# Fewer stages around the latent heads, a norm inside the projections, and a state space whose spans run two chunks ahead

## What is computed

```
# block one, state space mixer, 8 chunks of 128 tokens, 8 heads of 64
Lmat = exp(segsum(A))                                   # "spans"
y_diag = einsum(Cc, Bc, Lmat, X); y_off = einsum(Cc, prev, exp(a_cum))
y = (y_diag + y_off + d_skip * xs) * silu(z)
y = y * rsqrt(mean(y^2) + eps) * norm_w
# block two, run twice (2 layers)
xn = rms_norm(h, attn_norm); proj = xn @ w_in           # 1024 x 2208
q = (rms_norm(c_q, q_norm) @ w_uq)                      # latent attention, 6 heads of 64 + 32
kv = (rms_norm(c_kv, kv_norm) @ w_ukv)
q_pe = apply_rope(q[..., 64:]); o_b = softmax(q k^T * scale) v
h = h + concat(rms_norm(o_a), rms_norm(o_b), rms_norm(o_c)) * gn @ w_out
h = h + expert_choice_ffn(rms_norm(h, ffn_norm), ...)
```

## Time and profile before

| | us |
|---|---|
| median of 3 runs | 4294.49 |
| range of the runs | 4283.99 to 4298.66 |
| the profiled execution, own time | 4293.83 |
| its span | 4292.1 |
| PE busy | 3480.9 (81%) |
| DVE busy | 2808.4 (65%) |
| ACT busy | 1915.9 (45%) |
| mean granted clock of PE | 0.898 of full |

### The profile page before, as it was taken

One profiled execution on the slowest core, in us unless ns is written; L12 is line 12 of the kernel. 1 busy time (PEld: TensorE's weight loads), 2 busy tenths in 40 slices (PEclk: granted clock), 3 DMA queues, 4 the chain that ended last, 5 costly groups with the idle time before them and its releaser, 6 DMA issues. The chain is left out here.

```text
span 4292.1 us, 54019 instructions
## 1 busy us (share of the span) xinstructions
PE 3480.9 (81%) x18170; PEld 2563.5 (60%) x18170; DVE 2808.4 (65%) x4432; ACT 1915.9 (45%) x3024; POOL 513.8 (12%) x353
## 2 busy tenths in 40 slices
PE   7991559858880999698939999959978985799995
PEld 3440336746660786366828888848654664688884
DVE  1798346469995318365389999822554655899995
ACT  0100235126653126344327777622453531677774
POOL 0001200015553100100001111100001000011110
PEclk9995669969995999899969999979988997899997
DMA  3000000346624210001249999821100023799996
GB/s 120 23 0 11 6 1 2 109 187 260 253 88 171 77 50 3 20 1 60 104 164 376 384 385 385 334 97 49 27 10 11 1 96 126 281 384 383 383 384 242
DMA packets 122011, 649.31 MB, mean 151 GB/s; under 512 B 14176, under 2 KB 22752, under 8 KB 69856
## 3 DMA queue, kind: packets, MB, share of 16 engines
q1 hardware_dynamic: 101376, 572.44, 34.4%
q0 software_dynamic: 15984, 58.20, 4.7%
q10 hardware_dynamic: 4464, 16.25, 0.9%
HBM read 584.46 MB, written 62.39 MB: 151 GB/s over the span
## 5 line engine op out<-in xcount | busy, mean ns | idle before, releaser
L2950 DVE TENSOR_TENSOR low_ring<-mix,high_ring 128x2048 fp32r<-128x2048 f32 x256 | 576.6, 2284 | 41.3 <-ACT high_ring L2899 41.3
L2899 ACT ACTIVATE high_ring<-mix 128x2048 fp32r<-128x2048 f32 x256 | 477.8, 1937 | 130.8 <-PEq L122 130.8
L2840 PE MATMUL ps<-high_ring,x_high 128*128 128x512 f32 x1024 | 410.1, 400 | 14.9 <-DVE low_ring L2950 7.6
L2841 PE MATMUL ps<-low_ring,x_high 128*128 128x512 f32 x1024 | 401.1, 392 | 0.0
L2842 PE MATMUL ps<-high_ring,x_low 128*128 128x512 f32 x1024 | 400.6, 391 | 0.0
L2950 DVE TENSOR_TENSOR low_ring<-more_raw,high_ring 128x2048 fp32r<-128x2048 f32 x128 | 290.1, 2286 | 27.9 <-ACT high_ring L2899 27.9
L2899 ACT ACTIVATE high_ring<-more_raw 128x2048 fp32r<-128x2048 f32 x128 | 246.5, 1926 | 0.0
L2840 PEld LDWEIGHTS ps<-high_ring,x_high 128*128 128x128 f32 x1024 | 193.1, 189 | 78.9 <-DVE low_ring L2950 20.5
L2842 PEld LDWEIGHTS ps<-high_ring,x_low 128*128 128x128 f32 x1024 | 193.1, 189 | 41.4
L2841 PEld LDWEIGHTS ps<-low_ring,x_high 128*128 128x128 f32 x1024 | 193.3, 189 | 37.7
L2840 PE MATMUL ps<-high_ring,h_high 128*128 128x512 f32 x512 | 205.2, 401 | 0.0
(11 more groups left out here) (451 smaller groups left out, 8141.3 us busy)
## 6 DMA issues: line engine op xcount, KB each, us to landing
mix<-in_expert_units SPq DMA_DIRECT2D x256, 1024.0 KB, 8.0
more_raw<-in_expert_units SPq DMA_DIRECT2D x128, 1024.0 KB, 8.5
raw_experts<-in_expert_units SPq DMA_DIRECT2D x16, 3072.0 KB, 10.6
expert_out<-out ACTq DMA_DIRECT2D x31, 512.0 KB, 2.6
w_mix<-in_w_out SPq DMA_DIRECT2D x12, 1024.0 KB, 6.2
mix<-in_w_turned SPq DMA_DIRECT2D x20, 512.0 KB, 3.8
mix<-residual SPq DMA_DIRECT2D x8, 1024.0 KB, 8.2
mix<-residual SPq DMA_DIRECT2D x16, 512.0 KB, 3.3
```

The lines of the kernel that those rows point to most:

```text
L2840: nc.tensor.matmul(ps[:, bank, :], left_high, high, start=first, stop=False)
L2841: nc.tensor.matmul(ps[:, bank, :], left_high, low, start=False, stop=False)
L2899: nc.scalar.activation(w_high[:, n % RING, :], raw[n % RAW_UNITS], ACT.Copy).then_inc(high_ready, 1)
L2950: nc.vector.tensor_tensor(w_low[:, n % RING, :], raw[n % RAW_UNITS], w_high[:, n % RING, :].bitcast(F32), ALU.subtract).then_inc(low_ready, 1)
```

## The change

One edit in each of these places:

- State space: PE makes the spans of chunk c + 2 at the end of chunk c, and the pairs' first part of chunk c + 1 at its start; DVE writes `a_upto` two chunks ahead and `pairs` (now two buffers) one chunk ahead; the state product comes ahead of the outer one. The gates' Silu moves to ACT's start in `convolve`, the gating product and the square into the chunk loop, and the separate last stage goes.
- `project_two` takes in the norm, the transposes and the split: rows come tile by tile into the place of `feats`, each tile is squared, rooted, scaled by root and a gain row, turned, and split. Groups of the first two units are interleaved so that the first two need only tiles 0 to 3.
- `latent_heads` replaces five stages: norm, transposes, products for q, k and v and the rotary turn of q, in two halves of 512 tokens, over six PSUM banks, with all its DMAs issued at its start.
- `mix_out_square`: the gain row and the first two weight units are loaded during `attend_latent`, into the upper part of the old `qk` tile (now split in `body` and `tail`); the first weight unit is split ahead of the second tile's norm. There and in `mix_out_norm` the first product group waits for the first weight unit at its start and for the second only halfway (`halfway`).

```diff
-def split_products(nc, out, pairs):
+def split_products(nc, out, pairs, halfway=None):
...
+        if halfway is not None and 2 * n == len(terms):
+            halfway()
...
-                pe.wait_ge(low_ready, 2 * h + 2)
+                pe.wait_ge(low_ready, 2 * h + 1)
```

On ACT in `convolve`; on PE and on DVE in `state_space`:

```diff
+            for c in range(T):
+                nc.scalar.activation(z[:, c, :], z[:, c, :], ACT.Silu)
...
+                span(0)
+                inside(0)
+                span(1)
+                for c in range(T):
+                    if c + 1 < T:
+                        inside(c + 1)
...
+                    if c + 2 < T:
+                        span(c + 2)
...
+                steps_upto(0)
+                steps_upto(1)
+                pairs_of(0)
+                for c in range(T):
+                    if c + 2 < T:
+                        steps_upto(c + 2)
+                    if c + 1 < T:
+                        pairs_of(c + 1)
...
+                    dve.wait_ge(y_ready, c + 1)
+                    nc.vector.tensor_tensor(y, y, z[:, c, :], ALU.mult).then_inc(gated, 1)
```

On ACT in `mix_out_square` (DVE alike); then the groups, PE and DVE of `project_two`:

```diff
             group_square(0)
             group_root(0)
+            weights_of(0)
             group_square(1)
             group_root(1)
-            weights_of(0)
...
+    groups = [(0, 0), (1, 0), (0, 1), (1, 1)]
...
+            for t in range(5):
+                split_tile(t)
...
+                pe.wait_ge(split_low, T if g < 2 else 2 * T)
...
+                if g == 0:
+                    split_tile(5)
+                    split_tile(6)
+                if g == 1:
+                    split_tile(7)
...
+            for t in range(T):
+                norm(t)
+                if t >= 1:
+                    split_of(t - 1)
+                if t == 4:
+                    split(1)
```

PE in `latent_heads`, and the loads that now run beside `attend_latent`:

```diff
+            for g, (kind, s, i) in enumerate(ring):
+                if g == place["query", 0, 0]:
+                    pe.wait_ge(w_in, 32)
+                fill(g)
+                if g == place["query", 0, 0]:
+                    pe.wait_ge(tables_in, 48)
+                if kind == "query" and i >= 2:
+                    turn_query(s * H + i - 2)
+                if kind == "key" and i in (1, 3):
+                    turn_query(s * H + H - 2 + i // 2)
...
+                attend_latent(book, ps, ident, q, k, v_mla, mix, MLA_D ** -0.5,
+                              [(gain_row[:, :], A["group_rows"][bass.ds(layer, 1)].broadcast_to([P, D])),
+                               (w_next[:, 0], A["w_out_2"][mine][:, 0:4, 0:HALF]),
+                               (w_next[:, 1], A["w_out_2"][mine][:, 4:8, 0:HALF])])
```

More of the change, by code:

```diff
@@ L2442, in project_two @@
     loads_to = [sum(1 for v, _ in loads if v <= u) for u in range(len(units))]
[L2443 removed]
+    groups = [(0, 0), (1, 0), (0, 1), (1, 1)]
+    groups += [(u, part) for u, (kind, _) in enumerate(units) if u >= 2
+               for part in range(T if kind == "rows" else 2)]
     groups_to = [sum(1 for v, _ in groups if v <= u) for u in range(len(units))]
@@ L2657, in _, with square @@
-            for t in range(T):
-                act.wait_ge(full, g + 1)
-                nc.scalar.activation(v[:, t, :], ps[:, g % 8, 0:H * HD], ACT.Copy).then_inc(read, 1)
-                g += 1
+            def square(t):
+                for j, (a, b) in enumerate(SEGMENTS):
+                    if t >= 2:
+                        act.wait_ge(squares, 2 * (t - 2) + j + 1)
+                    nc.scalar.activation(junk[:, t % 2, a:b], lat[:, t, a:b], ACT.Square, scale=(b - a) ** -0.5,
+                                         accum_out=ss[:, t, j:j + 1]).then_inc(squares, 1)
@@ new lines, in _ @@
+            for t in range(4):
+                square(t)
+            for t in range(4, 6):
+                square(t)
+            roots_of(0)
+            for t in range(6, T):
+                square(t)
+            roots_of(1)
+            act.wait_ge(gain_in, 16)
+            for g in range(len(ring)):
+                take(g)
+        @block.gpsimd
+        def _(pool):
+            pool.wait_ge(tables_in, 48)
+            for n in range(2 * H):
+                s, h = divmod(n, H)
+                half = tile(s, HALF)
+                pool.wait_ge(read, place["query", s, h] + 1)
+                if n >= 2:
+                    pool.wait_ge(rotated, n - 1)
+                nc.gpsimd.tensor_tensor(by_cos[0:MLA_D, n % 2, :], q[0:MLA_D, h, half], cos[0:MLA_D, half],
+                                        ALU.mult).then_inc(cos_done, 1)
@@ L2662, in _, with scale @@
         @block.vector
         def _(dve):
+            chain = Chain(dve, steps)
+            def scale(s):
+                some = slice(4 * s, 4 * s + 4)
+                dve.wait_ge(squares, 8 * s + 8)
+                nc.vector.tensor_scalar(ss[:, some, :], ss[:, some, :], RMS_EPS, None, ALU.add).then_inc(means, 1)
+                dve.wait_ge(roots, s + 1)
+                chain.step(nc.vector.reciprocal(root[:, some, :], root[:, some, :]))
+                for t in range(4 * s, 4 * s + 4):
+                    for j, (a, b) in enumerate(SEGMENTS):
+                        last = nc.vector.tensor_scalar(lat[:, t, a:b], lat[:, t, a:b], root[:, t, j:j + 1], None, ALU.mult)
+                last.then_inc(scaled, 1)
```

405 lines of the change are left out of this document (257 added, 148 removed).

## The result

The changed kernel takes 4131.05 us (median of 4 runs, 4129.44 to 4137.72) against 4291.89 us (4 runs, 4283.99 to 4298.66): a ratio of 0.9629, 95% interval 0.9608 to 0.9649, so some 160 us less. Forecast were 4148 us and a gain of 145.9, range 4125 to 4181.

What follows compares the result with a forecast made beforehand. Bound by engine-to-engine chains cut by stage boundaries, except PE-bound projection products: 49.6 + 19.6 + 64.0 + 10.0 + 2.7 = 145.9 off 4293.8 gives 4148 us, own range 4136 to 4160, wider range 4125 to 4181.

Steps and rivals of the forecast that it cites:

- the rival at 4130: Whole program: PE keeps the full clock and POOL does not disturb, cycle 7.6, latents at their bound; 4130 us, chance 0.12.
- State space, 49.6 forecast: State space with gates and norm: 140.0 us become 90.4 as next chunk's span and Exps run beside this one's sums.
- the cycle: State space chunk loop: 9.6 us from span to span, five more spans making 48.0 us.
- its stated bound of 60: State space: gain of 60 us if the cycle is at its bound of 7.6 us; 30 at 13.5.
- the bound of 7.6: State space: PE's work per chunk at the full clock, 7.6 us, with a span of 4.2 us.
- 7.4: State space: DVE's path per chunk, with waits for Exps and crossings; POOL's disturbance of 1 to 2 us came on top.
- The rival of the low clock (4167): State space: PE stays at the low clock, 13.5 us a chunk, 19.5 us more; program 4167 us, chance 0.16.
- Projections, 9.8 a layer forecast: Projections: first product 15.7 us earlier, less 5.9 given back, leaves 9.8 us a layer, 19.6 for two.
- tile pace: Projections' lead: DVE sets the pace of norming and splitting, 3.5 us a tile.
- Given back inside the products: Projections: transposes between groups, a 1.6 us wait at group 3 and 1.0 for paired chunks cost 5.9 us a layer.
- Latent heads, 32.0 forecast: Latent stage: 28.9 us shorter, plus 3.1 from attend_latent starting at full clock; 32.0 a layer, 64.0 for two.
- Output projections, 5.0 forecast: Block two's output projection: first product at 2018.2 instead of 2023.1; 5.0 us a layer, 10.0 for two.

Runs made afterwards that it cites:

- e8: The changed kernel itself, run again unaltered: median of 5 4129.75 us, ratio to the kernel before 0.9613.
- e4: Changed kernel with an extra POOL product in state space chunks 2 to 5 and the old order of the projections' groups: 4141.8 us.
- e12: Changed kernel with idle PE products in state space, projections and latent stage, block two's output projection waiting for both weight units first: 4126.36 us, ratio to before 0.9601.
- e10: Changed kernel, but in both output projections the first group of each half waits for both weight units at its start: 4121.48 us.

## Why the prediction was right, and where it was off

The time lies in the stated range (4125 to 4181) and every part moved the way that was forecast. But it lies below the forecast's own 4136 to 4160, and about 1 us from the rival at 4130 (chance 0.12), in which PE keeps the full clock and POOL does not disturb. The first half of that rival is what happened; the second isn't. Some of the nearness is luck: the parts gained 21.9 us more than their sum, and the stages that the change doesn't touch took 11.6 of it back.

- **State space, 49.6 forecast, 61.9 measured.** The start (third span done at 488.0, 20.0 us; 21.5 forecast) and the end (22.7 us from the last span; 20.9 forecast, the low clock of the last products not seen) were within 2 us, with opposite signs. The term that was mis-sized is the cycle, 9.6 us forecast and 7.1 measured: five of them make 12.6 us, all of the miss, and the gain is above its stated bound of 60. On PE the bound of 7.6 was itself too long: a span's four products take 3.6 us from start to start, not 4.2, since each record ends after the next product has begun (starts 0.9 us apart, records of 1.0 to 1.1). On DVE I added POOL's disturbance to 7.4. DVE's period with the disturbance in it is 7.46: 5.8 of work and 1.5 behind POOL (a_upto 2.06 for 1.22, `state_new` 1.07 for 0.42). The waits for the Exps and the crossings, 1.6 us in my 7.4, were gone: DVE had other work. And I put PE at the low clock for part of the cycle, where its 7.05 us leave it no rest and the clock stayed up.
- **The rival of the low clock (4167)** did not come: from 488.0 to 523.4 PE is never idle. The Trainium skill (TensorE: Matmul & The Clock Gate, HAM oscillation) speaks of waits in each tile of a loop. Here it agrees where such a wait is left (2.14 us a chunk in the run with a_upto early, clock 0.79), and doesn't apply where none is.
- **DVE and POOL.** a_upto takes 1.8 to 2.1 us for 1.22 beside POOL's products from the fourth on. That agrees with the Trainium skill (SBUF — State Buffer, Who interferes with whom), and so does DVE's extra product of two SBUF tiles, which took 1.53 us for 0.69.
- **Projections, 9.8 a layer forecast, 13.4 and 12.7 measured.** The first product came 16.7 us earlier (15.7 forecast; tile pace 3.0, not 3.5). Given back inside the products were 3.3 us and not 5.9, though the wait of 1.66 and the transposes (1.0 a tile) were there. The products ran at a clock of 1.00 and not 0.99, which is up to 1.9 us of the difference; the rest I have not taken apart.
- **Latent heads, 32.0 forecast, 30.3 and 30.8 measured.** The stage is 63.5 us (62 forecast), with the mechanism as described. What the sum lacked is the low clock behind the transposes: the first twelve query records take 6.53 us, the same twelve of the second half 5.36. `attend_latent` gained 2.6 and not 3.1.
- **Output projections, 5.0 forecast, 8.6 measured in each layer.** The lead is 5.6 us shorter (5.0 forecast). The other 3.0 are the clock: 2.0 behind the lead, 0.9 at the end. In block one 2.9 us of lead became 1.4 of stage in this pair of traces, by the same means the other way: 9 products at the low clock for 7, and an end 1.1 us longer. In e8 it was 2.6 us, about what was forecast, and over eleven traces the stage takes 138.6 to 140.6 us with the old code and 135.7 to 137.5 with the changed one. What was off is that I let an earlier first product count one for one, with no term for the clock, which moves such a stage by as much as the term itself.

## What to carry to other kernels

Look for the wait inside each turn of a loop, and ask whether the next turn's work can stand in it on every engine: the gain was order plus clock, and the clock came without a trick once no wait was left. For the period of such a loop take the largest engine's work, with what two engines cost each other in it, and add no waits for which another turn's work is there. Read every engine's own period, too: where two differ (7.05 and 7.46 us here), the slower one is using up a head start, and a longer loop may end at its pace (an estimate, not run here). A gain or loss of 3 to 6 us in a PE-bound stage that follows a change elsewhere can be the moment at which the clock moves; compare the granted clock of lead and end before giving it a cause, and trust it only if it is there again when something else is changed too, or in another trace of the same kernel.

## What the hardware showed that I had not expected

The same stage, with the same code and the same lead of 12.8 us, took 129.9 and 136.1 us in two kernels that differ only ahead of it: clock 0.99 and 0.97 in the products, 0.94 and 0.63 in the light routing products at its end. In those two kernels both layers agree to 0.2 us, but in e4 they took 134.2 and 131.1, with the same code and the same waits. Why the moments differ stays open. The clock also fell while PE had had no longer pause than one of 0.47 us: the last 32 records of routing products took 6.85 us in the kernel before, in the changed one and in e12, and 3.92 in e10, which has the same pause.
